# A 192-byte gap in the on-chip memory map of a two-block transformer kernel

## The chip, the cores and the metric

The kernel runs on one core of one Trainium2 chip. The metric is the device time of one execution in microseconds (us). Before the change it is 2586.84 us, the median of 3 runs (2583.38 to 2588.46).

## The reference

The program is one chain of two blocks on 512 tokens of width 1024, all in 32-bit floats. The first block has two layers with a context stream of 256 tokens beside the 512 in its first layer (768 columns in all). The second block has two layers on 512 tokens alone. Almost all arithmetic is products of an activation matrix with a weight matrix:

```python
# first block, per layer (x: 512 tokens; xc: 256 context tokens, first layer only)
px = (rmsnorm(x, norm1_g[l]) * (1.0 + sc1) + sh1) @ w_in[l] + b_in[l]
...
x = x + g1 * (y_x @ w_out[l])
x = x + g2 * swiglu(rmsnorm(x, norm2_g[l]) * (1.0 + sc2) + sh2, w_gu[l], w_down[l])
...
def swiglu(h, w_gu, w_down):
    gate, up = jnp.split(h @ w_gu, 2, axis=-1)
    return (jax.nn.silu(gate) * up) @ w_down
...
# second block, per layer
h = mixer_a(x, a_w_in[j], a_w_out[j], cos, sin)      # or mixer_b
x = layer_norm(DEEPNORM_ALPHA * x + h, ln_g[i], ln_b[i])
gate = jax.nn.sigmoid((x @ ple_w_gate[i]).astype(jnp.float32))
x = (x.astype(jnp.float32) + gate * (p[i] @ ple_w_proj[i]).astype(jnp.float32)).astype(x.dtype)
```

## The kernel before

**A product.** Activations lie transposed: 128 features on the partitions, tokens along the row. Each operand is split into an upper part that the fast matmul type (`FP32R`) holds exactly and the rest. One weight tile has 8 steps of 128 input features; a step (`gemm_step`, L459 to L468) multiplies upper by upper (L463), upper weight by lower activation (L464) and lower weight by upper activation (L466). The activation is the moving operand, 512 columns at a time, and the weight tile of 128x128 is loaded into the array ahead of every matmul. A step on 768 columns has six matmuls, three of 512 and three of 256 columns.

**Weights.** SP streams weight tiles into a ring of four buffers `raw`. POOL (`split_weights`, L442 and L444, in one stretch ACT and POOL by `split_lower`, L457) makes `w_hi` (two buffers) and, in place over `raw`, `w_lo`. PE waits for the halves of a tile as they come and for the bank that it accumulates in.

**Activations.** Three pairs are multiplied with streamed weights. `XH`/`XL` hold the input of every product but those named next (in the second block `XH2`/`XL2`, which lie inside the same bytes). `HH`/`HL` hold the hidden values of the feed-forward part, for the down product, in both layers of the first block. `YH2`/`YL2`, called YH and YL by the profile and the title's list, are used in the second block: the output projection of mixer A, and all of mixer B's input projections. A fourth pair, `PH`/`PL` (L837 to L839), is multiplied with `PWH`/`PWL`, weights that stay in place.

**Addresses.** The program puts each tile at a byte address of its own choice. `place` takes the next free address, rounded up to 32 bytes, or the address that it is given. The lines of the change stand in this order, and what lies behind `XL` all counts on from `cursor`:

```python
raw = [place(f"raw{i}", [P, KT * P]) for i in range(RING)]
w_hi = [place(f"w_hi{i}", [P, KT, P], FP32R) for i in range(2)]
...
XH = place("XH", [P, KT, T], FP32R)
XL = place("XL", [P, KT, T], FP32R)
...
tri = place("tri", [P, 2, P])
...
HH = place("HH", [P, 8, T], FP32R, addr=work)
HL = place("HL", [P, 8, T], FP32R, addr=work + 8 * T * 4)
...
YH2 = place("YH2", [P, KT, SEQ], FP32R)
```

Here is how the addresses come out, each modulo 256. Call the first weight buffer's r. `raw` and `w_hi` are multiples of 256 bytes long, so all weights, upper and lower, are at r, and so is every step's slice of 512 bytes. Up to `X` come `Z` (12288 bytes, no remainder), `TH` (3136 bytes, remainder 64), `ident` and `ones` (no remainder) and two small ones (32 bytes each): `X`, `XH`, `XL` and the tile behind them, `tri`, are at r+128. `X2`, `XH2` and `XL2` begin whole multiples of 16384 bytes into `XH`. `YH2` stands behind `B2`, which begins where `tri` does and is 12480 bytes long (remainder 192): r+64. `work`, where `HH` and `kfm` begin, is 17856 bytes behind `tri` (remainder 192): r+64 too, with `HL`, `YL2`, the attention tiles `SM` and `PT`, and `PH`, `PL`, `PWH` and `PWL`. A step's slice of an activation begins a multiple of 1024 bytes further, so these remainders hold for every matmul. Modulo 512, `HH` and `HL` are 256 bytes apart from `YH2` and `YL2`, before and after the change.

**Order of work.** Each engine's program is written out by hand with semaphores; no scheduler decides anything.

Of the kernel before, what the change touches and what calls it, by code (L numbers as in the profile page):

```python
# [20 lines left out]
P = 128  # L21
# [181 lines left out]
def build_program(nc, xT, cT, cb_d, pc_d, fin_d, srow_d, consts_d, sguw_d, wg_d, wmod_d, win_d, wout_d, wgu_d, wdn_d,  # L203
# [4 lines left out]
    def place(name, shape, dt=FP32, addr=None):  # L208
        size = 4
        for s in shape[1:]:  # L210
            size *= s
        if addr is None:
            addr = cursor[0]
            cursor[0] += size + (-size) % 32
        assert addr + size <= nc.sbuf_usable_end, (name, addr + size, nc.sbuf_usable_end)
        addr_of[name] = addr
        return nc.alloc_sbuf_tensor_at(name, shape, dt, offset=addr)

    stack = ExitStack()
    with stack:  # L220
# [14 lines left out]
        XH = place("XH", [P, KT, T], FP32R)  # L235
        XL = place("XL", [P, KT, T], FP32R)

        tri = place("tri", [P, 2, P])
        mskd = place("mskd", [P, 2, P])
        mskr = place("mskr", [P, 2, P], FP32R, addr=addr_of["mskd"])  # L240
# [2786 lines left out]
```

## Time and profile before

| | |
|---|---|
| runs | 2583.38, 2586.84 and 2588.46 us; median 2586.84 us |
| span of the profiled execution | 2586.4 us |
| PE busy | 2522.5 us, 14594 matmuls |
| DVE, ACT, POOL busy | 1386.4, 776.3 and 1544.1 us |
| the 16 DMA engines | 255.57 MB, 99 GB/s on the mean |

The page gives no other time for the profiled execution than its span, which is 0.4 us under the median of the runs. A matmul's duration in the profile reaches from its start until its results are written, and the next matmul starts before that. So durations overlap, and the pace of PE is read from the starts in the timeline. There are 7848 matmuls of 512 columns and 2544 of 256 columns with streamed weights.

### The profile page before, as it was taken

The numbers are of one execution on the slowest core, as the hardware profiler recorded it, in microseconds if no ns is written. First come the engines' busy times: TensorE is split into PE (matmuls) and PEld (weight loads), VectorE is DVE, ScalarE is ACT, GpSimd is POOL, SyncE is SP. The second block draws the span as 40 slices with busy tenths as digits, with TensorE's granted clock in tenths as the row PEclk, the third lists the DMA queues.
The fourth block names the chain that finished last, engine by engine and source line by source line (L and its number), as shares of the span: only waits on it lengthen the run. The fifth ranks groups of instructions, "written<-read, shape, count | busy, mean of one in ns | idle before, by whom it ended". The sixth has DMA issues, their size and how long they took to land.

```text
span 2586.4 us, 39643 instructions
## 1 busy us (share of the span) xinstructions
PE 2522.5 (98%) x14594; PEld 2083.7 (81%) x14594; DVE 1386.4 (54%) x2065; ACT 776.3 (30%) x1620; POOL 1544.1 (60%) x1625
## 2 busy tenths in 40 slices
PE   6999999999999999999999999999999999999999
PEld 4888988888888886888788887778888888777876
DVE  5864556742853758726433333444444545556754
ACT  3224353111111123244321212222222222443544
POOL 3433245765766665543777777776666676556563
PEclk9999999999999999999999999999999999999999
DMA  7341142332333322121233232433333333323231
GB/s 280 107 155 41 34 179 86 127 130 65 122 130 98 119 60 69 58 66 42 83 96 94 93 98 82 130 106 100 91 103 96 93 103 94 98 73 98 83 106 65
DMA packets 79264, 255.57 MB, mean 99 GB/s; under 512 B 9872, under 2 KB 13712, under 8 KB 78864
## 3 DMA queue, kind: packets, MB, share of 16 engines
q1 hardware_dynamic: 63136, 213.21, 25.8%
q10 hardware_dynamic: 15984, 40.40, 5.1%
q8 instruction: 94, 1.54, 0.3%
q14 instruction: 50, 0.41, 0.1%
HBM read 236.28 MB, written 2.10 MB: 92 GB/s over the span
## 4 chain that ended last, share of the span: by engine, by line
PE 88%; DVE 4%; issue 3%; POOL 2%; ACT 2%; DMA 1%; SPq 0%; ACTq 0%; POOLq 0%; DVEq 0%
PE PS L463 21%; PE PS L466 21%; PE PS L464 21%; PE PS L1668 4%; PE PS L1670 4%; PE PS L1669 4%; PE PS L725 1%; POOL w_lo L444 1%; PE PS L714 1%; PE PS L708 1%; DMA raw<-in_wout 1%; PE PS L1524 1%; POOL w_hi L442 1%; DVE Z L2425 1%; DVE XL L2432 1%
## 5 line engine op out<-in xcount | busy, mean ns | idle before, releaser
L444 POOL TENSOR_TENSOR w_lo<-raw,w_hi 128x512 fp32r<-128x512 f32 (+1 forms) x606 | 880.5, 1453 | 50.6
L463 PE MATMUL PS<-XH,w_hi 128*128 128x512 f32 (+1 forms) x2080 | 782.7, 376 | 16.5 <-DVE XL L2432 3.3
L464 PE MATMUL PS<-XL,w_hi 128*128 128x512 f32 (+1 forms) x2080 | 755.6, 372 | 0.0
L466 PE MATMUL PS<-XH,w_lo 128*128 128x512 f32 (+1 forms) x2080 | 707.2, 373 | 0.0
L437 POOL TENSOR_TENSOR word<-ones 128x1 f32<-128x1 f32 x303 | 93.7, 309 | 869.4 <-PE PS L466 544.2
L463 PEld LDWEIGHTS PS<-XH,w_hi 128*128 128x128 f32 x2080 | 392.2, 189 | 118.6 <-issue 9.3
L442 POOL TENSOR_SCALAR w_hi<-raw 128x512 fp32r<-128x512 f32 (+1 forms) x606 | 482.0, 795 | 0.0
L464 PEld LDWEIGHTS PS<-XL,w_hi 128*128 128x128 f32 x2080 | 392.4, 189 | 70.0
L466 PEld LDWEIGHTS PS<-XH,w_lo 128*128 128x128 f32 x2080 | 362.5, 188 | 55.1
L1668 PE MATMUL PS<-XH,w_hi 128*128 128x512 f32 (+1 forms) x640 | 230.9, 361 | 8.4 <-DVE XL L2432 8.4
L1670 PE MATMUL PS<-XH,w_lo 128*128 128x512 f32 (+1 forms) x640 | 224.9, 351 | 0.0
L1669 PE MATMUL PS<-XL,w_hi 128*128 128x512 f32 (+1 forms) x640 | 224.8, 351 | 0.0
L2530 DVE TENSOR_TENSOR X<-X,Z 128x768 f32 (+3 forms) x60 | 86.0, 1433 | 228.6 <-ACT Z L2051 216.9
L463 PE MATMUL PS<-HH,w_hi 128*128 128x512 f32 (+1 forms) x528 | 187.6, 355 | 3.6 <-DVE HL L2896 3.6
L464 PE MATMUL PS<-HL,w_hi 128*128 128x512 f32 (+1 forms) x528 | 179.4, 354 | 0.0
L2494 DVE CUSTOM_DVE_ANT_0 cprod<-modv,cb 128x1024 f32<-128x1024 f32 x96 | 164.2, 1710 | 18.0 <-DMA modv<-in_wmod 15.1
L2891 DVE SCALAR_TENSOR_TENSOR Z<-TH,Z 128x768 f32<-128x768 f32 (+1 forms) x44 | 50.0, 1136 | 207.5 <-ACT Z L2032 206.4
L466 PE MATMUL PS<-HH,w_lo 128*128 128x512 f32 (+1 forms) x528 | 158.8, 355 | 0.0
L457 POOL TENSOR_TENSOR w_lo<-raw,w_hi 128x512 fp32r<-128x512 f32 x56 | 83.6, 1512 | 106.3 <-ACT w_hi L1051 84.9
L951 ACT ACTIVATE Z<-PS 128x512 f32<-128x512 f32 x99 | 58.7, 594 | 292.3 <-PE PS L466 279.5
L1668 PEld LDWEIGHTS PS<-XH,w_hi 128*128 128x128 f32 x640 | 121.5, 190 | 27.5 <-issue 9.6
L1670 PEld LDWEIGHTS PS<-XH,w_lo 128*128 128x128 f32 x640 | 121.3, 190 | 17.3
(346 smaller groups left out, 3507.0 us busy)
## 6 DMA issues: line engine op xcount, KB each, us to landing
raw<-in_wgu SPq DMA_DIRECT2D x88, 512.0 KB, 3.5
raw<-in_wa SPq DMA_DIRECT2D x80, 512.0 KB, 3.5
modt<-in_wmod SPq DMA_DIRECT2D x48, 512.0 KB, 9.9
raw<-in_win SPq DMA_DIRECT2D x48, 512.0 KB, 3.5
modv<-in_wmod ACTq DMA_DIRECT2D x48, 512.0 KB, 4.7
raw<-in_wdn SPq DMA_DIRECT2D x32, 512.0 KB, 3.6
QS<-Z ACTq DMA_DIRECT2D x96, 128.0 KB, 2.6
raw<-in_wout SPq DMA_DIRECT2D x16, 512.0 KB, 3.5
```

What stands on the lines that cost most here:

```text
L437: pool.tensor_tensor(word[:, 0:1], ones[:, 0:1], ones[:, 0:1], ALU.mult)
L442: pool.tensor_scalar(hi, src, 1.0, 0.0, ALU.mult, ALU.add).then_inc(s_hi, 1)
L444: pool.tensor_tensor(lo, src, hi.bitcast(FP32), ALU.subtract).then_inc(s_split, 1)
L457: pool.tensor_tensor(w_lo[s % RING][:, ks, :], src, w_hi[s % 2][:, ks, :].bitcast(FP32), ALU.subtract).then_inc(s_split, 1)
L463: pe.matmul(acc(s)[:, a:b], hi, rh[:, i, a:b], start=i == 0, stop=False)
L464: pe.matmul(acc(s)[:, a:b], hi, rl[:, i, a:b], start=False, stop=False)
L466: last = pe.matmul(acc(s)[:, a:b], lo, rh[:, i, a:b], start=False, stop=i == k - 1)
L1668: pe.matmul(out, hi, XH[:, i, a:b], start=first, stop=False)
L1669: pe.matmul(out, hi, XL[:, i, a:b], start=False, stop=False)
L1670: return pe.matmul(out, lo, XH[:, i, a:b], start=False, stop=i == KT - 1)
L2494: last = dve.tensor_tensor_reduce(out=cprod[:], in0=modv[slots + u][:], in1=cb[:, n, :], scale=0.5, scalar=0.0, op0=ALU.mult, op1=ALU.add, ...
L2530: dve.tensor_tensor(x, x, Z[:, s % 4, 0:w], ALU.add).then_inc(s_used, 1)
```

## The change

One line places a tile of 192 bytes, which nothing reads or writes, between `XL` and `tri`. Everything that is allocated behind `XL` moves up by 192 bytes; everything up to `XL` stays. No instruction is added, taken away or moved: the five engines have the same instructions in the same order, with other addresses.

```diff
         XH = place("XH", [P, KT, T], FP32R)
         XL = place("XL", [P, KT, T], FP32R)
 
+        place("lead", [P, 48])
         tri = place("tri", [P, 2, P])
         mskd = place("mskd", [P, 2, P])
```

Modulo 256, `HH`, `HL`, `YH2` and `YL2` go from r+64 to r, where the weights are. `XH` and `XL` stay at r+128. `PH`, `PL`, `PWH` and `PWL` go from r+64 to r together, as do `kfm`, `qfm`, `tho`, `vtm`, `SM` and `PT`. `tri`, `B2`, `KB` and `ST0` go from r+128 to r+64. `ident`, `ones` and `Z` stay, at r+64, r+64 and r.

## Rows read from the trace of the kernel before

**Rows 1.** Page, part 1, busy time and share of the span, and PEclk of part 2.
```profile
PE 2522.5 (98%) x14594; PEld 2083.7 (81%) x14594; DVE 1386.4 (54%) x2065; ACT 776.3 (30%) x1620; POOL 1544.1 (60%) x1625
...
PEclk9999999999999999999999999999999999999999
```

**Rows 2.** Page, part 4, the chain that ended last, by engine and line.
```profile
PE 88%; DVE 4%; issue 3%; POOL 2%; ACT 2%; DMA 1%; SPq 0%; ACTq 0%; POOLq 0%; DVEq 0%
```

**Rows 3.** Busy time by stretch: layers 1 and 2 of the first block; mixers A and B.
```profile
core 0: us, PE busy (x) PEld busy (x) DVE busy (x) ACT busy (x) POOL busy (x), PEclk, DMA share, GB/s
430.00:1000.00 570.00, 561.84 (x3153) 486.90 (x3152) 332.83 (x347) 113.70 (x166) 369.75 (x339) 0.99 0.32 106
1340.00:1650.00 310.00, 304.60 (x1305) 244.90 (x1304) 108.29 (x92) 63.70 (x103) 240.79 (x281) 1.00 0.30 92
2200.00:2260.00 60.00, 58.25 (x329) 45.93 (x322) 32.94 (x45) 26.27 (x52) 34.86 (x33) 1.00 0.32 105
...
2345.00:2480.00 135.00, 133.42 (x862) 107.93 (x861) 101.32 (x303) 66.47 (x208) 71.61 (x80) 1.00 0.27 78
```

**Rows 4.** Groups of PE by form: count, busy us, mean ns, idle before; upper times upper.
```profile
L463 PE MATMUL PS<-XH,w_hi 128*128 128x512 f32 x1664 | 665.3, 400 | 16.5 <-DVE XL L2432 3.3 <-ACT TH L2353 2.6 <-DVE XL L1310 2.2
...
L463 PE MATMUL PS<-HH,w_hi 128*128 128x512 f32 x352 | 138.0, 392 | 3.6 <-DVE HL L2896 3.6
...
L463 PE MATMUL PS<-YH,w_hi 128*128 128x512 f32 x216 | 86.8, 402 | 0.8 <-POOL w_lo L457 0.8
...
L463 PE MATMUL PS<-HH,w_hi 128*128 128x256 f32 x176 | 49.7, 282 | 0.0
```

**Rows 5.** Timeline of PE: start us, duration us; XH, 512 columns, first and 43rd.
```profile
1425.34 0.40 PE L463 MATMUL PS<-XH,w_hi 128*128 128x512 f32 x1
...
1435.10 0.40 PE L463 MATMUL PS<-XH,w_hi 128*128 128x512 f32 x1
```

**Rows 6.** Timeline of PE: HH, 512 columns, first and 52nd.
```profile
1505.03 0.39 PE L463 MATMUL PS<-HH,w_hi 128*128 128x512 f32 x1
...
1516.70 0.39 PE L463 MATMUL PS<-HH,w_hi 128*128 128x512 f32 x1
```

**Rows 7.** Timeline of PE: YH, 512 columns, first and 46th.
```profile
2242.46 0.39 PE L463 MATMUL PS<-YH,w_hi 128*128 128x512 f32 x1
...
2252.76 0.39 PE L463 MATMUL PS<-YH,w_hi 128*128 128x512 f32 x1
```

**Rows 8.** Timeline of PE: PH and PL with weights in place, first and twelfth.
```profile
2253.45 0.39 PE L837 MATMUL PS<-PH,PWH 128*128 128x512 f32 x1
...
2255.94 0.39 PE L839 MATMUL PS<-PH,PWL 128*128 128x512 f32 x1
```

**Rows 9.** Timeline of PE: the same pair behind other work, second and seventh.
```profile
2266.74 0.39 PE L838 MATMUL PS<-PL,PWH 128*128 128x512 f32 x1
...
2267.89 0.40 PE L837 MATMUL PS<-PH,PWH 128*128 128x512 f32 x1
```

**Rows 10.** Timeline of PE: HH, steps on 768 columns, start of the first and twelfth.
```profile
575.70 0.39 PE L463 MATMUL PS<-HH,w_hi 128*128 128x512 f32 x1
...
587.14 0.39 PE L463 MATMUL PS<-HH,w_hi 128*128 128x512 f32 x1
```

**Rows 11.** Timeline of PE: XH, steps on 768 columns, start of the first and fourth.
```profile
686.52 0.39 PE L463 MATMUL PS<-XH,w_hi 128*128 128x512 f32 x1
...
689.67 0.39 PE L463 MATMUL PS<-XH,w_hi 128*128 128x512 f32 x1
```

**Rows 12.** Timeline of PE: 256 columns with 16-column weights, first, and what follows the third.
```profile
1001.34 0.28 PE L1592 MATMUL PS<-XH,wgh 128*16 128x256 f32 x1
...
1001.68 0.39 PE L1592 MATMUL PS<-XH,wgh 128*16 128x512 f32 x1
```

**Rows 13.** Groups of PE by form: transposes of SM and of Z through ident.
```profile
L725 PE MATMUL PS<-ident,SM 128*128 128x128 f32 x256 | 33.4, 273 | 0.3 <-DVE SM L1238 0.2
...
L1557 PE MATMUL PS<-ident,Z 128*128 128x128 f32 x68 | 9.5, 274 | 0.0
```

## The prediction

> **What bounds the kernel now.** I read the page first, then the chain, then the stretches, then the groups by form and at last the timeline of PE. PE is busy for 98% of the span, at the full granted clock in each of the 40 slices [rows 1], and 88% of the chain that ended last runs through it [rows 2]. Every time that PE's pace changes by, the span changes by, where PE has no gaps. By stretch [rows 3]: in the two where HH and HL are used, PE is busy 561.84 of 570 us and 304.60 of 310 us, with POOL at 65% and 78%. There PE alone sets the time. Around mixer A's output projection it is 58.25 of 60 us. In mixer B, PE is busy 133.42 of 135 us, but DVE 101.32 us, and PE goes to and fro between weights and attention.
>
> The change alters neither an instruction nor its order, so the one question is whether PE's pace depends on addresses. Busy time can't say it, since durations overlap; the starts can. XH: from the first to the 43rd start 9.76 us, so 42 matmuls of 512 columns at 232.4 ns [rows 5]. HH: 51 in 11.67 us, 228.8 ns [rows 6]. YH: 45 in 10.30 us, 228.9 ns [rows 7]. These are three long runs of the same instruction with the same form, weights streamed by the same ring, clock at its upper level of 2.4 GHz. HH and YH lie in different regions and serve different blocks, yet have one pace; XH has another. What HH and YH share, and XH has not, is the distance from the weights modulo 256: 64 bytes, against 128. (Modulo 512 HH and YH differ, as HH's tiles and YH's start 256 bytes apart there; so 256 is the period that these rows bear out.)
>
> The case that the change makes, distance 0, is in the trace too. PH and PL lie at the same remainder as PWH and PWL. Their first run of twelve has eleven intervals in 2.49 us: 226.4 ns [rows 8]. So distance 128, 64 and 0 give 232.4, 228.8 and 226.4 ns. But the same pair does not run so from the start: behind other work it has five intervals in 1.15 us, 230.0 ns, with single ones from 0.23 to 0.24 us [rows 9]. It needs some matmuls to fall into step, at most about ten in this trace. In long runs, I take it, the settled pace counts.
>
> **The change, part by part.** The sum is made against the profiled span of 2586.4 us, 0.4 us under the median of 2586.84 us; a difference of this size is carried over to the median as it is.
>
> 1. *HH and HL, steps on 512 columns (second layer).* The group has 352 matmuls of 512 columns for each of the three products and 176 of 256 columns [rows 4]. Each step on 768 columns has one of either, so 176 steps are mixed and 352 - 176 = 176 are pure: 528 matmuls. From 228.8 to 226.4 ns is 2.4 ns: **-1.3 us**. Ends: if they never settle, 230.0 ns, +0.6 us; if they went to XH's pace, +3.6 ns, +1.9 us.
>
> 2. *HH and HL, mixed steps (first layer).* Eleven steps in 11.44 us: 1040 ns a step [rows 10]. XH's mixed steps are at 3.15 / 3 = 1050 ns [rows 11]. At distance 0 no row shows a matmul of 256 columns with whole weights. The nearest is one that loads 16-column weights, so that hardly any weight read lies beside it: three in 0.34 us, 113 ns [rows 12]. That is half of 226.4. I read 226.4 and 113 ns as what the moving operand alone needs, and a settled distance 0 as a state where the weight load adds nothing to it. Then a step is 3 x 226.4 + 3 x 113.2 = 1019 ns, 21 ns less: 176 x 21 = **-3.7 us**. Ends: 0 if the shorter matmuls keep the pair from settling; +10 ns a step, +1.8 us, at XH's pace. I take the first, as the two rows that it rests on agree to a nanosecond.
>
> 3. *YH and YL.* 216 x 3 = 648 matmuls of 512 columns [rows 4], of which 8 tiles x 8 steps x 3 = 192 are mixer A's output projection, nearly in one run: 192 x 2.4 = **-0.5 us**. The other 456 are mixer B's, in runs of 6 to 24 between transposes and scores, much of it at DVE's pace. Half would settle, half not: -2.4 or +1.2 ns each, so between -1.1 and +0.5 us. I take **0**.
>
> 4. *Settling.* Six stretches of HH and two of YH start behind other work: 8 x 10 matmuls x 3.6 ns: **+0.3 us**.
>
> 5. *What moves along.* PH and PWH move together. Transposes of SM get a distance of 64 from ident, where they had none. Transposes of Z through ident have that distance now and take 274 ns on the mean, against SM's 273 ns [rows 13]. For 256 + 112 transposes that is +0.4 us at most, and I take **0**. The attention tiles of the first block keep their distances from one another. No load grows, and no wait is added. DVE, ACT and POOL address moved tiles too. Their rows show no price of an address, and beside PE at 98% they would need microseconds in one place to matter: 0, with 1 us either way.
>
> 6. *What is late next.* PE asks for a weight tile some 58 ns sooner in each 24 matmuls (24 x 2.4), of 5.5 us. POOL is at 78% in the tightest of these stretches, so it has over 1 us a tile left. Nothing takes the gain back.
>
> Sum: -1.3 - 3.7 - 0.5 + 0.3 = -5.2 us. I give **2581.7 us**, which is 0.2% under 2586.84.
>
> **A rule that speaks against it.** The rows say that the pace differs by address: 232.4 against 228.8 ns [rows 5, 6]. The Trainium skill, "TensorE: Matmul & The Clock Gate", section "Step-by-step: what each phase is for", says that PE reads the moving operand and the next weights through two independent ports, and that loading the next weights takes no read bandwidth from the running matmul. By that, where a tile lies could not matter, and the sum would be 0: 2586.8 us. The trace does not agree so far; the rule makes the third rival below.
>
> **The rivals.**
>
> *A, the forecast: distance 0 settles in pure and mixed steps.* For it: rows 8 and 12. Against it: there are only eleven settled intervals in the row, and none in a mixed step. 2581.7 us.
>
> *B, it settles in pure steps alone.* In mixed steps, matmuls of two lengths alternate, and the start of each shifts the next against its weight load. Then part 2 falls away: -5.2 + 3.7 = -1.5 us, 2585.3 us. For it: the unsettled run [rows 9] shows that a pair at distance 0 can stay out of step for several matmuls.
>
> *C, the address is not the cause.* XH's pace could come from what else goes on in its stretches, and PH's from its weights not being streamed. 2586.8 us. Against it: PE's pace in XH's row belongs to a stretch where POOL streams weights just as it does in HH's [rows 3, 5, 6].
>
> *D, distance 0 collides.* Weight load and moving operand start at the same place of the 256 bytes within nanoseconds of each other. If that makes each wait for the other at every start, and the run of PH was short and lucky, the pair stays out of step for good. The place is every matmul with HH or YH; it decides as soon as the unsettled state is more frequent than two in three (230.0 against 226.4 ns, with 228.8 to beat). Priced at the worst long run that the trace has, XH's: (528 + 648) x 3.6 ns = 4.2 us, and 176 x 10 ns = 1.8 us. 2586.84 + 6.0 = 2592.8 us, slower. At the pace of row 9 it would be under 2 us.
>
> *E, the gap does something elsewhere* (DVE or ACT on moved tiles, or a stage that starts sooner and so meets its data better): a few us either way.
>
> **How the numbers follow.** A measurement of this kernel can tell about 0.2%, 5.2 us, from no change; the three runs alone span 5.1 us. A has 0.57, B 0.14, C 0.12, D 0.12, E 0.05. A lies on the bound itself: half of it counts as faster, half as the same. B and C are the same. D is beyond the bound where it has its full price: 0.08 slower, 0.04 the same. E: 0.04 faster, 0.01 slower. So faster 0.28 + 0.04 = 0.32, slower 0.08 + 0.01 = 0.09, the same 0.59. For the range: A with a run's scatter of 2.5 us reaches down to 2579, and the rest of the gain that part 3 could have (1.1 us) takes it to 2578. Upward B and C lie inside, and half of D's price with the scatter is 2586.84 + 3.0 = 2590.
>
> **What would show it.** In the profile after: starts of HH in a long pure run 226 to 227 ns apart, and of YH in mixer A's output projection the same; XH's still at 232.4 and mixed steps of XH at 1050 ns. HH's mixed steps at 1020 ns show A, at 1040 ns B. All three at their old paces show C, and 230 ns or more show D. PE's busy share stays at 98%. The forecast is wrong in its root if HH's starts don't move while the addresses did, and wrong in its sum if they move and the span doesn't: then another engine, POOL first, must have taken PE's place in these stretches.

## The result, and the profile after

The changed kernel takes 2589.8 us (median of 19 runs, 2585.1 to 2593.1) beside 2586.5 us before (19 runs, 2583.3 to 2588.6): a ratio of 1.0015 [1.0008, 1.0022]. That is 3.3 us slower, less than the 0.2% that the prediction named as the bound. The profiled span went from 2586.4 to 2588.8 us, +2.4 us. The forecast was 5.2 us faster. The sign was wrong; the time lies at the upper end of the range.

The page after the change, busy times and the engines of the chain that ended last:

```profile
PE 2525.5 (98%) x14594; PEld 2084.0 (81%) x14594; DVE 1393.5 (54%) x2065; ACT 776.8 (30%) x1620; POOL 1547.4 (60%) x1625
...
PE 74%; POOL 13%; issue 7%; DVE 3%; ACT 1%; DMA 1%; POOLq 0%; SPq 0%; ACTq 0%; DVEq 0%
```

PE is as full as before [rows 1]. The chain looks like news: POOL went from 2% to 13% [rows 2]. It isn't. A second profile of the changed kernel gives this chain:

```profile
PE 88%; DVE 4%; issue 3%; POOL 2%; ACT 2%; DMA 1%; SPq 0%; ACTq 0%; POOLq 0%; DVEq 0%
```

So the chain's shares differ between two executions of one kernel, and POOL's 13% say nothing of the change. What decides is whether PE has gaps, and the busy time by stretch (columns as in [rows 3]) says that it has none that it had not before:

```profile
430.00:1000.00 570.00, 562.48 (x3138) 485.26 (x3136) 329.54 (x344) 111.59 (x164) 366.25 (x338) 0.99 0.32 106
1340.00:1650.00 310.00, 304.47 (x1307) 244.72 (x1307) 107.82 (x90) 63.28 (x103) 242.76 (x283) 1.00 0.31 93
2200.00:2260.00 60.00, 58.91 (x346) 46.91 (x345) 32.29 (x45) 26.66 (x54) 35.87 (x35) 1.00 0.33 106
2345.00:2480.00 135.00, 133.02 (x863) 107.89 (x864) 104.68 (x304) 66.35 (x207) 74.15 (x82) 1.00 0.27 77
```

In the first of them, layer 1, PE is busy 0.64 us longer in the same 570 us, and gets through 15 matmuls fewer there. So the pace has to be read, from starts. PE's timeline after the change, start and duration (the gemm lines 463, 464 and 466 of before are now 464, 465 and 467):

```profile
577.34 0.39 PE L464 MATMUL PS<-HH,w_hi 128*128 128x512 f32 x1
...
578.38 0.40 PE L464 MATMUL PS<-HH,w_hi 128*128 128x512 f32 x1
...
579.44 0.39 PE L464 MATMUL PS<-HH,w_hi 128*128 128x512 f32 x1
...
588.91 0.40 PE L464 MATMUL PS<-HH,w_hi 128*128 128x512 f32 x1
...
650.20 0.40 PE L464 MATMUL PS<-XH,w_hi 128*128 128x512 f32 x1
...
653.38 0.40 PE L464 MATMUL PS<-XH,w_hi 128*128 128x512 f32 x1
...
1425.21 0.39 PE L464 MATMUL PS<-XH,w_hi 128*128 128x512 f32 x1
...
1435.01 0.39 PE L464 MATMUL PS<-XH,w_hi 128*128 128x512 f32 x1
...
1505.19 0.39 PE L464 MATMUL PS<-HH,w_hi 128*128 128x512 f32 x1
...
1516.75 0.39 PE L464 MATMUL PS<-HH,w_hi 128*128 128x512 f32 x1
...
2242.13 0.39 PE L464 MATMUL PS<-YH,w_hi 128*128 128x512 f32 x1
...
2252.33 0.39 PE L464 MATMUL PS<-YH,w_hi 128*128 128x512 f32 x1
```

- Pure HH, 51 matmuls in 11.56 us: 226.7 ns, from 228.8 [rows 6]. Pure YH, 45 in 10.20 us: 226.7 ns, from 228.9 [rows 7]. Both have the settled pace of PH [rows 8], and hold it through the whole run.
- Pure XH, 42 in 9.80 us: 233.3 ns, beside 232.4 [rows 5], as before.
- HH's mixed steps, 11 in 11.57 us: 1052 ns, from 1040 [rows 10]. The first two take 1.04 and 1.06 us: short and long steps take turns.
- XH's mixed steps, three in 3.18 us: 1060 ns, beside 1050 [rows 11]. XH did not move.

From the starts of all undisturbed steps in the two traces (three matmuls a pure step, six a mixed one; over 160 steps in each mean):

| ns a step | HH mixed | HH pure | XH mixed | XH pure | YH pure |
|---|---|---|---|---|---|
| before | 1040.3 | 686.9 | 1052.2 | 698.1 | 686.8 |
| after | 1053.2 | 680.9 | 1059.2 | 698.5 | 683.2 |

So 176 mixed steps of HH cost 13 ns more each, +2.3 us; 176 pure ones bring 6 ns, -1.1 us; 216 of YH bring 3.6 ns, -0.8 us. XH's mixed steps in the stretch between layer 1's first two passes through HH (618 to 753 us, 128 steps) went from 1049 to 1060 ns: +1.4 us. Sum: +1.8 us, of 3.3 us between the medians [2.1 to 5.7]. Between these two profiles XH's stretch behind the second pass went from 1049 to 1060 ns as well, +1.1 us; the spans differ by 2.4 us. The experiments show that most of that stretch changes by chance.

### The profile page after: what moved, and what is told of

Same layout as the page of the kernel before. It is cut to its first block, busy times and chain, and to the rows that moved or that the text cites. A ratio compares the mean times of both kernels' runs of the same rounds, so it can differ in the third digit from the quotient of the medians.

```text
span 2588.8 us, 39643 instructions
## 1 busy us (share of the span) xinstructions
PE 2525.5 (98%) x14594; PEld 2084.0 (81%) x14594; DVE 1393.5 (54%) x2065; ACT 776.8 (30%) x1620; POOL 1547.4 (60%) x1625
## 4 chain that ended last, share of the span: by engine, by line
PE 74%; POOL 13%; issue 7%; DVE 3%; ACT 1%; DMA 1%; POOLq 0%; SPq 0%; ACTq 0%; DVEq 0%
PE PS L464 17%; PE PS L467 16%; PE PS L465 16%; POOL w_lo L445 8%; POOL w_hi L443 5%; PE PS L1669 4%; PE PS L1671 4%; PE PS L1670 4%; PE PS L726 1%; PE PS L715 1%; POOL word L438 1%; PE PS L709 1%; DVE XL L2433 1%; PE PS L1525 1%; DVE Z L2426 1%
## 5 line engine op out<-in xcount | busy, mean ns | idle before, releaser
L1670 PE MATMUL PS<-XL,w_hi 128*128 128x512 f32 (+1 forms) x640 | 224.9, 351 | 0.0
```

The costliest lines, as they stand in the source:

```text
L1670: pe.matmul(out, hi, XL[:, i, a:b], start=False, stop=False)
```

## The experiments

The theory after the result: a distance of 0 between moving operand and weights is good for pure steps and bad for mixed ones, and the two nearly cancel. The rivals: the loss comes from other buffers that moved, or from what differs between any two executions. No run changes an instruction's work, but for the two that reorder the matmuls of the mixed steps or cut HH's.

**One half at a time.** The first kernel puts HH and HL at distance 0 in layer 1 alone, the second in layer 2 alone, with YH and YL. Each layer gets its own placement:

```diff
-        HH = place("HH", [P, 8, T], FP32R, addr=work)
-        HL = place("HL", [P, 8, T], FP32R, addr=work + 8 * T * 4)
+        HHL = [place(f"HH{l}", [P, 8, T], FP32R, addr=work + (0, 64)[l]) for l in range(DEPTH)]
+        HLL = [place(f"HL{l}", [P, 8, T], FP32R, addr=work + 8 * T * 4 + (0, 64)[l]) for l in range(DEPTH)]
...
+        place("lead2", [P, 16])
```

That is the mixed half, made from the changed kernel (lead2 stands ahead of YH2 and takes YH and YL back to 64). The other half is made from the kernel before, with no lead, (0, 192) in both lists, and 48 words in lead2.

> Distance 0 for HH and HL in the first layer alone (steps on 768 columns); second layer and YH back at distance 64. Theory 1 (mixed steps at distance 0 cost 13 ns each, and they hand XH's mixed steps behind them to a slower repeating pattern): HH's mixed steps at 1053 ns, 176 x 13 ns = +2.3 us; XH's mixed steps at 1060 ns after every stretch of HH, +2.9 us; HH's pure steps at 687 ns. In all +5.2 us, about 2591.8 us against 2586.6. Theory 2 (XH's pattern changes from one execution to the next by chance): +2.3 us and XH's mixed steps at 1049 ns in some stretches. Theory 3 (the time is lost to another engine, POOL first, since its share of the chain grew): the mixed steps may be at 1053 ns, but the time does not follow their sum.

> Distance 0 for HH and HL in the second layer and for YH and YL; HH and HL of the first layer at distance 64 as in the kernel before. Theory 1: HH's pure steps at 680 ns instead of 687 (176 x 6 to 7 ns = -1.1 us), YH's steps at 683 ns (216 x 3.6 ns = -0.8 us), mixed steps of HH at 1040 ns and those of XH at 1049 ns behind them, as before. In all -1.9 us, about 2584.7 us. Theory 2: the same -1.9 us, with XH's mixed steps at 1060 ns in some stretches. Theory 3: the paces of PE change but the time stays within 0.5 us.

The mixed half: 2589.4 us against 2586.84, 1.0009 [1.0000, 1.0018]. Mixed HH 1053.2 ns, pure HH 686.9, YH 687.3. PE's timeline in it, three steps' starts:

```profile
577.35 0.39 PE L464 MATMUL PS<-HH,w_hi 128*128 128x512 f32 x1
...
578.39 0.40 PE L464 MATMUL PS<-HH,w_hi 128*128 128x512 f32 x1
...
579.45 0.39 PE L464 MATMUL PS<-HH,w_hi 128*128 128x512 f32 x1
```

The gaining half: 2584.93 us against the same 2586.84, 0.9995 [0.9986, 1.0004]. Mixed HH 1040.3 ns, pure HH 680.7, YH 683.3. The same view of it, the starts of the first and third of three mixed steps, then of three pure ones:

```profile
577.20 0.39 PE L463 MATMUL PS<-HH,w_hi 128*128 128x512 f32 x1
...
579.28 0.39 PE L463 MATMUL PS<-HH,w_hi 128*128 128x512 f32 x1
...
1504.66 0.39 PE L463 MATMUL PS<-HH,w_hi 128*128 128x512 f32 x1
...
1506.02 0.39 PE L463 MATMUL PS<-HH,w_hi 128*128 128x512 f32 x1
```

Two mixed steps take 2.08 us here and 2.10 us above; two pure ones 1.36 us, 680 ns each. Each pace goes with the address of its own operand, whatever the rest does: +2.6 us by one half, -1.9 us by the other. The first interval just touches no change and the second spans it; the paces are clear, each a mean of 167 steps or more. The +5.2 us of theory 1 did not come: XH paid only between the first two passes, not behind the second (1051 ns there). The halves add to +0.7 us, where the whole change gave 3.3; each has an interval of about 2.3 us either way, so the halves show whose pace goes with which address, and not the size of the total.

**The two kernels once more, unchanged.** This asks what differs between executions of one kernel.

> The kernel before once more, for a second profile. Theory 1: XH's mixed steps at 1060 ns ahead of the first stretch of HH and at 1049 ns behind it, as in the first profile. Theory 2: another division between 1049 and 1060 ns.

> The changed kernel once more, for a second profile. Theory 1: XH's mixed steps at 1060 ns in all stretches, HH's at 1053 ns. Theory 2: some stretches of XH at 1049 ns.

> The changed kernel once more, for the size of the loss and a third profile. From the paces in the profiles so far: HH's mixed steps +2.3 us, XH's mixed steps between the first two stretches of HH +1.4 us, HH's pure steps -1.1 us, YH -0.8 us: +1.8 us if XH's other mixed stretches are at 1049 or 1060 ns by chance as often as in the kernel before; up to +4.7 us if these are at 1060 ns in every execution.

One run of the kernel before took 2587.78 us, one of the changed kernel 2591.16; with more rounds the changed kernel took 2589.3 us against 2586.5 (11 and 15 runs), 1.0011 [1.0002, 1.0020]. HH's mixed steps are at 1040.2 ns in the kernel before, and at 1053.1 in both new profiles of the changed one. XH's are not so fixed. PE's timeline of the kernel before, second profile, in the stretch between HH's passes:

```profile
650.18 0.40 PE L463 MATMUL PS<-XH,w_hi 128*128 128x512 f32 x1
...
651.23 0.39 PE L463 MATMUL PS<-XH,w_hi 128*128 128x512 f32 x1
...
652.26 0.40 PE L463 MATMUL PS<-XH,w_hi 128*128 128x512 f32 x1
...
653.32 0.40 PE L463 MATMUL PS<-XH,w_hi 128*128 128x512 f32 x1
```

The steps take 1.05, 1.03 and 1.06 us, where after the change each of three took 1.06. At distance 128 a mixed step has two repeating patterns, with means of 1049 and 1060 ns, and PE keeps the one that it is in until something interrupts it. Layer 1 has three long stretches of XH. The one ahead of HH (414 to 552 us, 128 steps) and the one behind HH's second pass (819 to 925 us, 96 steps) had either pattern in profiles of the same kernel: that is up to 1.4 and 1.1 us of scatter. The one between goes with HH: 1049 ns in three of three profiles with HH at 64, 1060 in five of five with HH at 0. (In one profile each, 1049 with HH at 96 and 1060 with HH at 192.)

What tells the stretches apart is a pause. PE runs through the one between without one. The one ahead of HH has steps of up to 2.1 us near 425 us. In the one behind PE stops after 16 steps, in every profile; in that of the kernel before, at 836 us (waits of PE: us in total, times, longest):

```profile
PE PS L463 <- ACT TH L2353: 2.6, 1, 2.6
```

The granted clock is 0.51 there from 838.7 to 845 us, and when the pace is back the pattern can be another. In the 15 steps ahead of the pause the rule holds here too: 1048 ns with HH at 64 (three of three), 1060 with HH at 0 (five of five). Behind the pause either came with either address. So HH hands on a pattern, and XH pays 1.4 us for it in a place that the change didn't touch. (The mixed half pays it too.)

**XH at 64.** If the address is the cause, XH must follow it as well. `word` and `eps_c` are placed behind XL instead of ahead of X:

```diff
-        word = place("word", [P, 8])
-        eps_c = place("eps_c", [P, 2])
...
         XL = place("XL", [P, KT, T], FP32R)
+        word = place("word", [P, 8])
+        eps_c = place("eps_c", [P, 2])
```

> Against the kernel before, two small tiles move behind XL, so that X, XH and XL, and XH2 and XL2 with them, come to distance 64; HH and YH stay at 64. Theory 1 (the distance modulo 256 alone sets the pace of a step): XH's mixed steps at 1040 ns instead of 1049 or 1060 (672 x 9 to 20 ns = -6 to -13 us), all in one pattern in all stretches; its pure steps at 687 ns instead of 698 (1376 x 11 ns = -15 us). In all -21 to -28 us, 2559 to 2566 us. Rival (XH's pace comes from its region or from what runs beside it): XH's steps stay at 1049 to 1060 and 698 ns, no change within 2 us.

2568.94 us against 2586.34 (5 and 9 runs), 0.9932 [0.9919, 0.9946]: 17.4 us faster. XH's mixed steps fell from 1052 to 1040.2 ns, its pure ones from 698 to 687.5, just HH's and YH's paces at 64. PE's timeline, from the first to the fourth of XH's mixed steps, three in 3.12 us:

```profile
650.27 0.39 PE L463 MATMUL PS<-XH,w_hi 128*128 128x512 f32 x1
...
653.39 0.39 PE L463 MATMUL PS<-XH,w_hi 128*128 128x512 f32 x1
```

All three stretches now have one pattern. 394 undisturbed mixed steps x 12 ns and 1370 pure ones x 10.6 ns make 19.2 us by the steps. The spans of the two profiles differ by 20.0 us (2586.4 and 2566.4), the medians by a little less. Both lie under the 21 to 28 us expected, but the paces came as expected: the expectation had 672 mixed steps of XH, of which 256 (L1668 to L1670, most of them sent by `tile_part`) have their 512 columns and their 256 in separate runs, and three matmuls of 256 columns went from 357 to 350 ns only.

**Each operand at its better distance.** XH as in the run above, HH and HL at 64 in layer 1 and at 0 in layer 2, YH and YL at 0, and the second block's XH2 and XL2 at 0:

```diff
+        gt = place("gt", [P, NJ, 2, 2, HEADS])
+        word = place("word", [P, 8])
+        eps_c = place("eps_c", [P, 2])
...
+        HHL = [place(f"HH{l}", [P, 8, T], FP32R, addr=work + (0, 192)[l]) for l in range(DEPTH)]
...
+        place("lead2", [P, 16])
...
+        XH2 = place("XH2", [P, KT, SEQ], FP32R, addr=addr_of["XH"] + KT * SEQ * 4 + 192)
+        XL2 = place("XL2", [P, KT, SEQ], FP32R, addr=addr_of["XH"] + 2 * KT * SEQ * 4 + 192)
```

> Every pair at the distance that is best for its steps by the profiles so far: XH and XL of the first block and HH and HL of its first layer at 64 (the mixed steps), HH and HL of the second layer, XH2, XL2, YH and YL at 0 (pure steps). Theory 1: second block's XH at 680 to 682 ns a step instead of 698 (832 x 17 ns = -14 us), pure steps of XH in the first block at 687 (544 x 11 ns = -6 us), XH's mixed steps at 1040 (-6 to -13 us), HH's pure steps and YH -1.9 us. In all -28 to -35 us, 2552 to 2559 us. Rival (another engine takes PE's place where PE gets faster: POOL in the second block, DVE in mixer B): the steps are at these paces, but the time falls by less than 20 us and PE waits for POOL.

2562.43 us against 2586.34, 0.9908 [0.9893, 0.9923]: 23.9 us faster than the kernel before, and 6.5 us faster than the one with XH at 64. Mixed steps are at 1040.1 and 1040.3 ns, pure HH at 681.1, YH at 683.1, XH2 at 680 in its long runs. PE's timeline, six pure steps of XH2 in 4.08 us:

```profile
1800.61 0.39 PE L463 MATMUL PS<-XH,w_hi 128*128 128x512 f32 x1
...
1804.69 0.39 PE L463 MATMUL PS<-XH,w_hi 128*128 128x512 f32 x1
```

The gain is below the 28 to 35 us expected. In mixer A the second block's XH2 comes in runs of some 20 to 40 matmuls between attention, and the first steps of a run are at 690 to 697 ns before it is at 680: a run at 0 needs some matmuls to settle. But that is little: the mean over the undisturbed steps there is 682.0 ns, within the 680 to 682 expected. This expectation counted the 256 steps too high as well; what else is missing was not traced.

**Why mixed steps don't settle.** Two edits of the changed kernel. The first sends all three products of the 512 columns and then all three of the 256, so that the length changes twice in a step and not four times (six matmuls in one loop over `ranges(w)`, in place of two loops). The second cuts HH's mixed steps into nine matmuls of 256 columns, all of one length:

```diff
-            for a, b in ranges(w):
+            cut = [(0, 256), (256, 512), (512, T)] if rh is HH and w == T else ranges(w)
+            for a, b in cut:
...
```

> The changed kernel, with the six matmuls of a mixed step in another order: the three of 512 columns first, then the three of 256, so the length changes twice a step instead of four times. If it is the change of length that keeps distance 0 from settling, HH's mixed steps come down from 1053 ns to between 1019 and 1040 ns. If a matmul of 256 columns costs more at distance 0 by itself, they stay at 1050 ns or above. XH's mixed steps, at distance 128, move either way.

> The changed kernel, with HH's mixed steps cut into nine matmuls of 256 columns instead of three of 512 and three of 256. If distance 0 settles for any one length, they take 9 x 113.3 = 1020 ns a step. If matmuls of 256 columns do not settle at distance 0, they take 9 x 117 ns or more, 1053 ns and above.

The first: 2587.77 us in one run, HH's mixed steps 1050.0 ns. Its timeline shows three steps of 1.05 us:

```profile
576.95 0.40 PE L464 MATMUL PS<-HH,w_hi 128*128 128x512 f32 x1
...
580.10 0.40 PE L464 MATMUL PS<-HH,w_hi 128*128 128x512 f32 x1
```

Fewer changes of length save 3 of the 13 ns, so their number is not the main cause; why two lengths in turn do not settle at 0 stays open. (XH's mixed steps run in this order too, at 1055 ns in all three stretches.) The second: 2594.09 us in one run, a step 1079.8 ns. Its timeline, two steps of nine matmuls in 2.16 us:

```profile
577.02 0.28 PE L465 MATMUL PS<-HH,w_hi 128*128 128x256 f32 x1
...
579.18 0.28 PE L465 MATMUL PS<-HH,w_hi 128*128 128x256 f32 x1
```

Each matmul of 256 columns takes 120.0 ns, every one the same: this is a settled pace, and it isn't half of 226.7. The difference, 106.7 ns for 256 columns, is one column a clock at the upper level of 2.4 GHz. Taken off as such, 213.3 ns for 512 columns and 106.7 for 256, it leaves 13.3 ns at either length. A mixed step wholly in step would be 3 x 226.7 + 3 x 120.0 = 1040 ns, worked out from these two: what HH had before.

**Other distances.** Three kernels shift the same buffers by other amounts (here the first; the others differ in the numbers):

```diff
+        place("lead", [P, 32])
...
+        HHL = [place(f"HH{l}", [P, 8, T], FP32R, addr=work + (0, 96)[l]) for l in range(DEPTH)]
...
+        place("lead2", [P, 8])
```

The second has 8 words in lead, (0, 96) and 16 words in lead2. The third has no lead, (0, 192), and makes `eps_c` a part of `word`, so that all behind moves down by 32 bytes, XH too.

> Other distances from the weights: HH and HL at 192 in the first layer (mixed steps) and at 32 in the second (pure steps), YH and YL at 224, XH at 128 as before. If the cost depends on how far apart the two are, either way round, 192 is like 64 (mixed 1040 ns), and 32 and 224 lie between 0 and 64 (pure 680 to 687 ns). If it matters which of the two is ahead, 192 and 224 differ from 64 and 32: mixed at 1050 ns or more, pure at 690 ns or more.

> HH and HL at 96 in the first layer (mixed) and at 192 in the second (pure), YH and YL at 160, XH at 128. By distance alone: mixed between 1040 and 1052 ns, pure at 192 as at 64 (687 ns), at 160 as at 96, between 687 and 698 ns. By which is ahead: pure at 192 and 160 away from these by 5 ns or more.

> XH, XL, XH2 and XL2 at 96 (mixed and pure), HH and HL at 32 in the first layer (mixed) and at 224 in the second (pure), YH and YL at 32 (pure). By distance alone: XH's mixed steps between 1040 and 1052 ns and its pure ones between 687 and 698 ns; HH's mixed steps between 1040 and 1053 ns; pure at 32 and 224 alike, 680 to 687 ns. If XH's slower pace were its own and not its address, XH stays at 1049 to 1060 and 698 ns.

One run each: 2591.65, 2592.2 and 2597.05 us, beside 2586.5. PE's timeline of the second, two pure steps of HH at 192 in 1.40 us, where they took 1.36 at 0:

```profile
1505.24 0.39 PE L464 MATMUL PS<-HH,w_hi 128*128 128x512 f32 x1
...
1506.64 0.39 PE L464 MATMUL PS<-HH,w_hi 128*128 128x512 f32 x1
```

With all kernels together, ns a step by the distance from the weights modulo 256 bytes:

| distance | 0 | 32 | 64 | 96 | 128 | 160 | 192 | 224 |
|---|---|---|---|---|---|---|---|---|
| mixed (HH; at 96 HH and XH, at 128 XH) | 1053 | 1050 | 1040 | 1053 | 1049 or 1060 | not run | 1047 | not run |
| pure (HH, YH, XH) | 680 | 700 | 687 | 700 | 698 | 703 | 700 | 700 |

64 and 192 are equally far from the weights and yet differ, so it isn't the mere distance; a law that gives this table was not found. Among the pure steps only 0 and 64 beat 698. For the third kernel the paces give 176 x 9.6 ns (mixed HH), 176 x 13 (pure HH), 216 x 13.3 (YH) and 1370 x 2.3 (pure XH), 1.7 + 2.3 + 2.9 + 3.2 = +10.1 us, and +10.5 us was measured. That it comes so near is luck: for the first two the same working gives +7.6 (with the 1.4 us of XH's stretch between) and +8.0 us, and +5.1 and +5.7 were measured. Single runs of the kernel before lie between 2583.4 and 2589.1 us.

In all these runs the streamed weights stay in place, so for them the table can't tell the distance from the activation's own address modulo 256. PH and PWH can: the change moved both by 192 bytes, and their distance stayed 0. PE's timeline after the change, the same first run of twelve:

```profile
2255.73 0.39 PE L838 MATMUL PS<-PH,PWH 128*128 128x512 f32 x1
...
2258.23 0.39 PE L840 MATMUL PS<-PH,PWL 128*128 128x512 f32 x1
```

Eleven intervals take 2.50 us, where they took 2.49 before [rows 8]. At the address that PH had before, modulo 256, HH at distance 64 took 228.8 ns [rows 6]. So PH's pace stayed with the distance and not with the address; for streamed weights this was not run.

## Why the prediction was wrong

**Part 1 and part 3, pure steps: right.** 226.7 ns for HH and YH where 226.4 was taken, -1.1 and -0.8 us where -1.3 and -0.5 stood. The kernel with these alone was 1.9 us faster; -1.8 was forecast for the pair. YH in mixer B gained a little more than the nothing that it was given: the mean over all its runs is 683.2.

**Part 2, mixed steps: this is the step that failed.** It stood at -3.7 us and measured +2.3. It read 226.4 ns for 512 columns and 113 for 256 [rows 8, 12] as one rate, and took the agreement of the two for proof. Two errors lie in it. First, the settled cost at distance 0 is a fixed 13.3 ns over the columns at either length (226.7 and 120.0 ns): 113 came from matmuls that load 16-column weights, and is not what whole weights leave. With the right number even the best case of this part was 3 x 226.7 + 3 x 120.0 = 1040 ns: no gain was to be had. Second, the mixed steps don't settle; they alternate between 1043 and 1063 ns. The upper end in the working, XH's pace at +10 ns, was close to the 13 that came.

**Part 4, settling:** too small to be told apart; the means over all of the runs, settling included, are 680.9 and 683.2 ns a step. (The 0.4 us between span and median in the base of the sum compare two executions: a span lies 1.75 to 2.95 us below the time of its own execution, as 2588.8 below 2591.11 us in the profiled one after the change. The sum is a difference, so nothing hangs on it.)

**Part 5, what moves along: missed one thing.** XH's place and instructions didn't change, and yet a stretch of it pays 1.4 us for the pattern that HH hands on.

**Part 6, what is late next: nothing,** as said; PE stays full [rows 3].

**The rivals.** A is refuted: 1020 ns never came. B had the mechanism of the pure steps right (they alone settle), with a price of 0 for the mixed ones where +2.3 us was due. D said that the pair stays out of step for good, and that is what mixed steps do, near the price that it took (13 ns for its 10); pure ones don't. What came is B in layer 2 and D in layer 1, a mix that the prediction didn't have, though each stage's steps had rows of their own. C is refuted by the paces in both halves, and by XH at 64, which gained 17.4 us by address alone. E had no run to itself: in the mixed half the other tiles stay moved, and its +2.6 us is no more than HH's 2.3 and XH's 1.4 us make, so nothing is left that asks for it. The rule behind C is that weights and moving operand come through two independent ports and that a load takes no bandwidth from the running matmul (the Trainium skill, "TensorE: Matmul & The Clock Gate", section "Step-by-step: what each phase is for"). It does not make placement free here: the same matmuls on the same weights take 680 ns a step at distance 0 and 700 at 192. That the weight load and the moving operand meet is the reading nearest at hand; no run here shows what in the chip makes the address count.

**What stays open.** The steps account for 1.8 of the 3.3 us between the medians. The 15 steps of XH ahead of the pause add 0.2 us. The later comparison gives 2.8 us, with an interval of 0.5 to 5.2, and the two stretches of XH whose pattern changes from one execution to the next move a run by up to 1.1 and 1.4 us. The rest is within that, and nothing further was shown for it.

## What to carry to other kernels

Where PE is full for whole stretches and each matmul loads new weights, try the address of the moving operand against the weights' modulo 256 bytes, for each buffer and each shape of step by itself: here placement alone was worth 0.9%, and the change that moved two shapes together gave its gain back. Take the pace from starts, not from busy time or the chain, and from steps of the same shape; a rate carried over from a matmul with another load beside it can hide a fixed cost. When the paces of a kernel can differ in the same program, compare the profile of one kernel with itself before a microsecond is explained.

## What was not expected of the hardware

- A settled stream at distance 0 costs its columns and 13.3 ns a matmul, at 256 columns as at 512 (120.0 and 226.7 ns), at a granted clock of 1.00 in these stretches.
- The best distance depends on the lengths in the stream: 64 for mixed steps (1040 ns against 1053 at 0), 0 for pure ones (680 against 687).
- A stream of equal steps falls into a repeating pattern and keeps it for over a hundred steps, until PE pauses. At 128 there are two (1049 and 1060 ns): behind HH the pattern goes with HH's address, and after a pause of 2.6 us it can be another from one execution to the next. This makes up to 1.4 us of scatter in a stretch, and lets a moved buffer change the time of one that stays.
- The chain that ended last gave POOL 13% in one profile of the changed kernel and 2% in another, with spans of 2588.8 and 2589.4 us.
